# Squares and sums of each layer's first norm, and the first two slots of projection weights, moved in front of the barrier

## The reference, cut to what matters

```python
def rmsnorm(x, g):
    xf = x.astype(jnp.float32)
    y = xf * lax.rsqrt(jnp.mean(xf * xf, axis=-1, keepdims=True) + NORM_EPS)
    return (y * g.astype(jnp.float32)).astype(x.dtype)

for l in range(DEPTH):                                   # DEPTH = 2
    u, q, kc, vc, ks, vs, kw, vw, g = jnp.split(rmsnorm(x, norm_mix) @ w_in, IN_SPLITS, axis=-1)
    m = mix_output(s5_mixer(u, h0), gates, o_cmp, o_slc, o_win)   # state space group and sparse attention
    x = x + m
    x = x + swiglu_ffn(x)                                # norm_ffn, w_ffn_gate, w_ffn_up, w_ffn_down
```

## Time and profile before

| | us |
|---|---|
| median of 3 runs | 3360.0 (3359.72 to 3361.36) |
| the profiled execution, its own time | 3358.03 |
| its span, first to last instruction | 3356.5 |
| mean granted TensorE clock, as a share of full speed | 0.974 |
| PE busy | 3163.6 (94% of the span) |
| DVE busy | 1825.3 (54%) |
| ACT busy | 1209.5 (36%) |

### The profile page before, as it was taken

The page is one execution under the profiler, slowest core; times in us unless marked ns, Lnnn a source line. Parts: engine busy times, 40 slices in busy tenths (PEclk is TensorE's granted clock), DMA queues, the critical chain, the costliest instruction groups (busy, mean ns, idle before and its releaser), DMA issues. The chain is left out here.

```text
span 3356.5 us, 56753 instructions
## 1 busy us (share of the span) xinstructions
PE 3163.6 (94%) x22054; PEld 2848.1 (85%) x22054; DVE 1825.3 (54%) x2530; ACT 1209.5 (36%) x1483; POOL 313.4 (9%) x560
## 2 busy tenths in 40 slices
PE   7999998779999999999989999987799999999998
PEld 5777776569999999999967777765799999999998
DVE  6886565635444444444468856665354444444444
ACT  2112553523333333333321135534243333333333
POOL 0002233310000000000000022343100000000000
PEclk9999999889999999999989999988799999999999
DMA  5436366754444444444344363676544444444443
GB/s 198 172 141 251 110 202 218 226 204 165 159 173 156 169 164 161 155 170 157 119 166 165 142 238 123 204 232 212 201 159 167 165 160 173 152 175 150 171 154 128
DMA packets 141645, 579.79 MB, mean 173 GB/s; under 512 B 21506, under 2 KB 91043, under 8 KB 115491
## 3 DMA queue, kind: packets, MB, share of 16 engines
q1 hardware_dynamic: 105858, 472.62, 38.2%
q0 software_dynamic: 26816, 77.63, 6.8%
q10 hardware_dynamic: 8800, 27.40, 2.2%
HBM read 570.02 MB, written 24.18 MB: 177 GB/s over the span
## 5 line engine op out<-in xcount | busy, mean ns | idle before, releaser
L1100 PE MATMUL banks<-normed_hi,weights_hi 128*128 128x288 f32 x4224 | 1250.9, 296 | 6.5 <-DVE ffn_hidden L1480 3.4
L1100 PE MATMUL banks<-normed_lo,weights_hi 128*128 128x288 f32 x4224 | 1246.1, 295 | 0.0
L1100 PE MATMUL banks<-normed_hi,weights_lo 128*128 128x288 f32 x4224 | 1241.9, 294 | 0.0
L1480 DVE TENSOR_TENSOR weights_lo<-weight_slots,weights_hi 128x2048 fp32r<-128x2048 f32 x296 | 686.9, 2321 | 977.3 <-ACTq L1401 976.8
L1398 ACT ACTIVATE weights_hi<-weight_slots 128x2048 fp32r<-128x2048 f32 x296 | 566.7, 1915 | 1079.5 <-PE banks L1100 1077.8
L1100 PEld LDWEIGHTS banks<-normed_hi,weights_hi 128*128 128x128 f32 x4224 | 791.5, 187 | 8.6 <-issue 4.8
L1100 PEld LDWEIGHTS banks<-normed_hi,weights_lo 128*128 128x128 f32 x4224 | 795.5, 188 | 0.0
L1100 PEld LDWEIGHTS banks<-normed_lo,weights_hi 128*128 128x128 f32 x4224 | 792.9, 188 | 0.0
L698 PE MATMUL banks<-normed,weight_slots 128*128 128x288 f32 x1664 | 415.0, 408 | 0.0
L698 PEld LDWEIGHTS banks<-normed,weight_slots 128*128 128x128 f32 x1664 | 312.4, 190 | 97.2 <-issue 14.6
L895 PE MATMUL banks<-conv_high,conv_weights 128*128 128x508 f32 x1024 | 331.4, 405 | 15.3 <-DVE conv_low_b L1480 10.3
(11 more groups left out here) (313 smaller groups left out, 2810.5 us busy)
## 6 DMA issues: line engine op xcount, KB each, us to landing
weight_slots<-in_w_gu SPq DMA_DIRECT2D x88, 2048.0 KB, 7.4
weight_slots<-in_w_down SPq DMA_DIRECT2D x44, 2048.0 KB, 7.4
weight_slots<-in_w_in SPq DMA_DIRECT2D x28, 2048.0 KB, 8.8
arena<-in_cache_cmp SPq DMA_DIRECT2D x256, 128.0 KB, 4.2
arena<-in_cache_cmp POOLq DMA_DIRECT2D x256, 128.0 KB, 4.2
weight_slots<-in_w_out SPq DMA_DIRECT2D x16, 2048.0 KB, 7.7
out_win_kept<-in_win_rows ACTq DMA_DIRECT2D x32, 508.0 KB, 7.4
weight_slots<-in_w_glu SPq DMA_DIRECT2D x8, 1024.0 KB, 6.5
```

The lines of the kernel that those rows point to most:

```text
L1100: mm = pe.matmul(out, wt[:, hf, col], x[:, rhs + c, :], start=begin and c == 0 and i == 0, stop=hf == 1 and c == k - 1 and i == 2, skip_gr ...
L1480: return dve.tensor_tensor(out, a, b, op)
```

## The change

In the front block ACT now squares all 16 chunks, DVE adds them all to one chunk, and PE multiplies ones with that chunk into bank 0. SP issues the first two blocks of layer 0's `w_in` there too, and waits for both before the barrier. At the end of a layer's block ACT squares the second half right behind each of DVE's four additions, and PE sums the squares into bank 0 before the barrier; SP loads two blocks of `w_in` for the next layer as soon as the slots are free (after the last layer it loads blocks 0 and 1 once more, which nobody reads). At the start of a layer's block there is then no square, no sum and no load of the first two blocks; DVE waits for `params` alone, and SP only raises `full` for the two slots, since the barrier cleared the semaphores.

```diff
+    MIX_SQ = [SQ[:, :, :]] + [HC[:, 2 * j:2 * j + 2, :] for j in range(3)]
...
+    def late_square(act, j):
+
+        return act.activation(MIX_SQ[j], XT[:, SC + 2 * j:SC + 2 * j + 2, :], ACT.Square)
...
+            for s in range(2):
+                sp.dma_start(WR[:, s, :, :].rearrange("p k x -> p (k x)"), T["w_in"][s]).then_inc(full[s], 16)
             sp.wait_ge(S["consts_in"], 32)
             sp.wait_ge(S["x_in"], 16)
+            for s in range(2):
+                sp.wait_ge(full[s], 16)
...
             early_sum(dve)
+            for j in range(1, 4):
+                dve.wait_ge(S["mix_sq"], j + 2)
+                dve.tensor_tensor(MIX_SQ[0], MIX_SQ[0], MIX_SQ[j], ALU.add)
+                dve.drain()
+            for v in (MIX_SQ[0][:, 1, :], HC[:, SC, :]):
+                dve.tensor_tensor(MIX_SQ[0][:, 0, :], MIX_SQ[0][:, 0, :], v, ALU.add)
+                dve.drain()
+            dve.drain().then_inc(S["mix_var"], 1)
+
+        @block.tensor
+        def _(pe):
+            pe.wait_ge(S["consts_in"], 32)
+            pe.wait_ge(S["mix_var"], 1)
+            pe.matmul(bank(0)[:, 0:TOK], ones, MIX_SQ[0][:, 0, :], start=True, stop=True)
...
             early_squares(act).then_inc(S["mix_sq"], 1)
+            for j in range(4):
+                late_square(act, j).then_inc(S["mix_sq"], 1)
     nc.all_engine_barrier(sems_to_clear=range(handles[0].num, handles[-1].num + 1))
...
-                stream("w_in", J_IN, 14, peel=2)
+                for s in range(2):
+                    sp.drain().then_inc(full[s], 16)
+                stream("w_in", J_IN, 14, skip=1)
...
                 stream("w_down", J_DN, 2 * DR)
+                for s in range(2):
+                    sp.wait_ge(freed[s], (J_DN + 2 * DR - J_OUT) // 2)
+                    sp.dma_start(slot(s), row("w_in", 14 - 14 * lay + s)).then_inc(full[s], 16)
                 sp.wait_ge(S["win_copied"], 256)
+                for s in range(2):
+                    sp.wait_ge(full[s], 16 * ((J_DN + 2 * DR) // 2 + 1))
...
-                pe.matmul(bank(4)[:, 0:TOK], ones, HC[:, SC, :], start=True, stop=False)
-                for j in range(4):
-                    pe.wait_ge(S["mix_sq"], j + 1)
-                    for m in range(2):
-                        mm = pe.matmul(bank(4)[:, 0:TOK], ones, MIX_SQ[j][:, m, :], start=False, stop=j == 3 and m == 1)
-                mm.then_inc(S["mix_stat"], 1)
...
+                pe.wait_ge(S["mix_sq"], 1)
+                pe.wait_ge(S["down_evac"], 9)
+                pe.matmul(bank(0)[:, 0:TOK], ones, HC[:, SC, :], start=True, stop=False)
+                for j in range(4):
+                    pe.wait_ge(S["fn_sq"], 10 + j)
+                    for m in range(2):
+                        pe.matmul(bank(0)[:, 0:TOK], ones, MIX_SQ[j][:, m, :], start=False, stop=j == 3 and m == 1)
...
-                for j in range(4):
-                    act.activation(MIX_SQ[j], XT[:, SC + 2 * j:SC + 2 * j + 2, :], ACT.Square).then_inc(S["mix_sq"], 1)
...
                 early_squares(act).then_inc(S["fn_sq"], 1)
+                for j in range(4):
+                    act.wait_ge(S["down_evac"], 9 + j)
+                    late_square(act, j).then_inc(S["fn_sq"], 1)
...
-                norm_all(dve, "mix", lambda c: XT[:, c, :], lambda c: HC[:, c, :], C_MIX, KC, sums=1)
+                norm_all(dve, "mix", lambda c: XT[:, c, :], lambda c: HC[:, c, :], C_MIX, KC, stat=0, sums=0)
...
                 early_sum(dve)
+                dve.drain().then_inc(S["mix_sq"], 1)
                 down_add(1)
```

More of the change, by code:

```diff
@@ L626, in norm_var @@
             def norm_var(dve, n, k, stat, v, width):
-                dve.wait_ge(S[n + "_stat"], k)
+                if k:
+                    dve.wait_ge(S[n + "_stat"], k)
                 dve.tensor_scalar(v, stat, 1.0 / width, EPS, ALU.mult, ALU.add).then_inc(S[n + "_var"], 1)
@@ L639, in norm_all @@
             def norm_all(dve, n, src, dst, gain, count, stat=4, sums=None, cols=slice(0, TOK)):
-                norm_var(dve, n, sums or count, bank(stat)[:, cols], NV[:, 0, cols], count * P)
+                norm_var(dve, n, count if sums is None else sums, bank(stat)[:, cols], NV[:, 0, cols], count * P)
                 norm_recip(dve, n, 1, NV[:, 0, cols], NR[:, 0, cols], NV[:, 1, cols])
@@ L650, in build @@
             RSTD = HC[:, 0, :]
-            MIX_SQ = [SQ[:, :, :]] + [HC[:, 2 * j:2 * j + 2, :] for j in range(3)]
             SIG = [VRF[:, STEP * i:STEP * i + STEP].rearrange("p (m t) -> p m t", m=2) for i in range(2)]
```

## The result

The changed kernel took 3369.53 us (median of 7 runs, 3366.15 to 3373.12), the kernel before 3357.75 (7 runs, 3352.7 to 3361.36): **a ratio of 1.0032, interval 1.0022 to 1.0041**, slower by 0.3%. The profiled execution took 3368.1 with a span of 3366.6, 10.1 more than that of before.

What follows compares the result with a forecast made beforehand. Behind the first projection PE has no slack, so shifts there move the end. 12.8 - 4.4 + 0.5 + 2.9 - 5.4 + 2.9 = +9.3 on 3358.0 gives 3367.3; median 2.0 higher: 3369.3 us, range 3364.5 to 3375.5.

Steps and rivals of the forecast that it cites:

- The front barrier, +12.8: Front block: SP's wait for the early weights moves the barrier's last arrival from 14.7 to 27.5, +12.8 us.
- my "about 5 us" without the cover: Front block: the added squares and sums would cost about 5 us if SP's wait for weights did not hide them.
- my 27.5: Front block: predicted landing time of the two early weight loads, in us, setting the barrier's last arrival.
- The rival of a front at the best rate: Front block: everything moves at 442 GB/s, weights land at 24.4, sum +6.2, no measurable change; chance 0.20.
- `params`, -4.4 and -5.4: Barrier to DVE's norm: `params` lands sooner on idle DMA engines, gaining 4.4 us in layer 0, 5.4 in layer 1.
- my bound of 5.1: Layer 0, barrier to DVE's norm: largest gain allowed, 5.1 us, if `params` lands in 2.3 us.
- that rival: Start of both layers: `params` lands no sooner, its 6.5 us being the queue's own; sum +16.3, 3376.3; chance 0.10.
- my 3.0: Start of both layers: predicted time from issue to landing of the 31 KB `params` load, 3.0 us.
- The first projection, +0.5: Layer 0: PE idles longer beforehand, so its first projection takes layer 1's length, +0.5 us.
- The late sums, +2.9 twice: Seam between layers and end: PE's sums at full clock reach each barrier 2.9 us later than DVE's additions did.
- The rival at half clock: Seam and end: PE makes its late sums at half clock, twice 2.4 us more, +14.1, 3374.1; chance 0.06.
- The sum: Whole kernel: all terms from front, `params`, projection, seam and end together make it +9.3 us slower.

Runs made afterwards that it cites:

- Weights alone: Kernel before, plus only the early weight loads and SP's wait for them at the front barrier; squares and sums stay in the block: 3372.09 us, ratio 1.0046.
- sums alone: Changed kernel with the first two weight blocks loaded inside the layer's block again, only squares and sums ahead of the barriers: 3372.87 us, ratio 1.0049.
- runs with a busy PE: Changed kernel without front wait, `params` and half of `y` early, plus 12 or 8 unused PE products per layer start: 3352.17 and 3350.86 us.
- the run with 8 extra products: Changed kernel without front wait, `params` and first half of `y` early, plus eight unused PE products at each layer's start: 3350.86 us, ratio 0.9978.
- no wait and `params` early: Changed kernel without the front barrier's wait for weights and with `params` loaded ahead on SP's queue: 3356.91 us, ratio 1.0001.
- run 6: Not a run number: in "that run 6 rows", 6 counts PE rows; the run is no wait and `params` early, 3356.91 us.

## Why the prediction was right, point by point

**The front barrier, +12.8.** GpSimd's first issue moved from 17.13 to 30.49, +13.4, with SP's wait for the weights in front of it. Weights alone moved it by 13.7, sums alone by 5.2; my "about 5 us" without the cover was right. The landing, 27.9, was 0.4 us behind my 27.5: the bytes were through at 26.1, where I had 26.4, but the landing came 1.8 us behind them, not 1.1. The rival of a front at the best rate, with a landing at 24.4, falls: the stretches from 14 to 26 moved 417 GB/s on average.

The Trainium skill, page "DMA: Bandwidth & Descriptors", section "Where 436 GB/s comes from", gives 435 GB/s, which this rival's paragraph names as the ceiling, for the ports of SBUF, and says that transfers between HBM and SBUF, as these loads are, are bound at about 358. The measured 417 lies under the first and above the second.

**`params`, -4.4 and -5.4.** Measured 7.50 - 2.31 = 5.2 and 8.48 - 2.84 = 5.6: more than I took, in layer 0 by 0.1 us beyond my bound of 5.1, in layer 1 inside the bounds. Landing took 2.3 and 2.8 us on idle engines and 6.1 and 6.2 with the weights beside it (sums alone), so the 6.5 us were the engines' sharing, not the queue's own, and that rival falls.

The Trainium skill, page "DMA: Bandwidth & Descriptors", section "Anatomy of one DMA — SWDGE (gpsimd) path", gives an estimate of 2.1 us for this load (2.0 and its bytes at 436 KB per us). Of the two landing times, 2.3 lies nearer to it and 2.8 nearer to my 3.0; with weights alone it was 2.1 and 2.5. The 6.1 and 6.2 beside the weights lie outside it.

**The first projection, +0.5.** Layer 0 took 18.00 us instead of 17.35 (+0.65), but layer 1 17.30 instead of 17.84, a gain that I had not given. My reason, that PE idles longer, does not carry it: in layer 1 PE idled 13.50 us instead of 4.66 and the projection got shorter. By the runs with a busy PE both are a start at the lower clock, whose length varies from kernel to kernel; that the figure for layer 0 came out near was luck.

The Trainium skill, page "TensorE: Matmul & The Clock Gate", Part 1, says that an idle array is gated to 1.2 GHz and a busy one gets 2.4; the stretches of the run with 8 extra products agree, 0.50 behind the idle time and 1.00 once the extra products have run.

**The late sums, +2.9 twice.** Measured 2.93 at the seam and 3.0 at the end (14.76 against 11.74), at full clock: 12 rows took 3.07 us, against 4.75 in the earlier trace rows. The rival at half clock falls, and doubling the sums moved both ends by their length. SP's early loads were hidden, as forecast: issued at 1665.66 and 1678.29, they landed 7.4 and 7.5 us later, the second at 1685.8, before PE.

**The sum.** By places 8.5 us against my 9.3: the front barrier cost 0.6 more than I took and `params` gave 1.0 more, the projections 0.4 more, so the terms' errors partly cancel. The spans differ by 10.1, since this profile's two rests are 1.6 us longer; the medians differ by 11.8. 9.3 us would be a ratio of 1.0028, inside the interval, so the predicted 3369.3 and the measured 3369.53 agree more closely than the method can claim: I had started from a median of 3360.0, and with all runs that of before is 3357.75.

## What to carry to other kernels

When two things end at almost the same time, moving one gains little: here sums alone and weights alone each cost time, and only together did they take 5 us off the wait behind the barrier, so test the parts of such a change singly. Put a load in front of a barrier, but its wait where the data is used: waiting for it at the barrier held the next block up by 8.2 us. Without the wait 4.4 of them came back at the next step; most of the others went to `params`, which then shared the DMA engines with the load. Where an engine idles before a long run of products, look at the granted clock and the pace of that run's first microseconds, and count it in every gain that only lets the run start sooner.

## What was not expected of the hardware

The first projection of 64 rows took 15.68 to 15.76 us behind extra products and 17.30 to 18.79 behind an idle PE, with the same instructions; what sets it within the second range no run shows. In layer 0 the PEclk column shows 1.00 even where the rows come at half pace. In the run with no wait and `params` early (the first pair of figures in a stretch is PE's busy time and its rows):

```profile
28.00:30.00 2.00, 2.00 (x5) 1.38 (x5) 2.00 (x6) 0.00 (x0) 0.00 (x0) 1.00 0.94 354
...
34.00:36.00 2.00, 2.00 (x10) 1.58 (x9) 0.78 (x5) 0.85 (x2) 0.00 (x0) 1.00 0.01 4
```

In layer 1 of that run 6 rows per 2 us stand beside 0.50 (1694 to 1698). So in layer 0 the rows tell the clock and the column does not. Two further things stay open: 1.8 us between the last bytes of the weights and the end of the wait for them, and some 6 us from the last arrival at the loop's barrier to the first issue behind it (1690.96 to 1697.08 after, 1678.08 to 1684.29 before), which no run here took apart.
